# Four buffers of TensorE operands placed 64 bytes further along in SBUF

## The reference

```python
    h = rmsnorm(x, norm_ffn[l])
    gt, up = jnp.split(h @ w_ffn_in[l], 2, axis=-1)
    x = x + ((jax.nn.silu(gt) * up) @ w_ffn_out[l]).astype(x.dtype)
return rmsnorm(x, norm_final)
```

## The kernel before

| operand | role | before |
|---|---|---|
| `h_hi`, `h_lo` | moving | on the line |
| `t_hi`, `t_lo` | moving | on the line |
| weight rings `w_hi`, `w_lo` (sums, output weights) | stationary, then moving | on the line |
| `wa22` blocks, both sets (product 2) | stationary | on the line |
| `wa_lo`, set 0 | stationary | half off (`H + 8192`) |
| `wa_hi`, `wa_lo`, set 1 | stationary | half off (`H`, `H + 14464`) |
| `wa_hi`, set 0 | stationary | on the line (`Dd + 32768`) |
| `a_hi`, `a_lo` | stationary | on the line |

## Time and profile before

### The profile page before, as it was taken

How to read it: one execution, slowest core, us unless ns; L and a number is a source line. 1 busy time by engine, 2 the same in 40 slices (tenths; PEclk the granted TensorE clock), 3 DMA queues, 4 the chain that set the end, 5 groups by cost and what they waited for, 6 DMA issues and landing times.

```text
span 783.5 us, 12585 instructions
## 1 busy us (share of the span) xinstructions
PE 775.8 (99%) x4994; PEld 676.3 (86%) x4994; DVE 485.5 (62%) x920; ACT 327.2 (42%) x597; POOL 154.6 (20%) x111
## 2 busy tenths in 40 slices
PE   9999999999999999999999999999999999999996
PEld 7878899889878787788888988999999999888885
DVE  5935432555776767656625668898788876332347
ACT  5212055254446666653313624444444443222145
POOL 1300100000000000002200185876666650000000
PEclk9999999999999999999999999999999999999999
DMA  6941336250311111036331731334333335333302
GB/s 217 339 154 54 108 61 155 57 167 4 109 54 55 55 55 41 23 98 190 108 108 54 229 94 55 108 109 117 104 104 107 108 109 192 130 108 107 107 1 107
DMA packets 101286, 83.50 MB, mean 107 GB/s; under 512 B 16960, under 2 KB 94832, under 8 KB 101232
## 3 DMA queue, kind: packets, MB, share of 16 engines
q1 hardware_dynamic: 100992, 82.46, 35.2%
q10 hardware_dynamic: 240, 0.29, 0.1%
HBM read 77.44 MB, written 5.29 MB: 106 GB/s over the span
## 4 chain that ended last, share of the span: by engine, by line
PE 99%; DMA 0%; ACT 0%; DVE 0%; issue 0%; ACTq 0%; DVEq 0%
PE bank L1681 28%; PE bank L1682 28%; PE bank L1683 28%; PE bank L1914 2%; PE bank L1933 2%; PE bank L1901 2%; PE bank L1815 1%; PE bank L1856 1%; PE bank L1837 1%; PE bank L1778 1%; PE bank L1722 1%; PE bank L1705 1%; PE bank L1728 1%; PE bank L1928 1%; PE bank L1731 0%; PE bank L1868 0%
## 5 line engine op out<-in xcount | busy, mean ns | idle before, releaser
L1028 DVE TENSOR_TENSOR w_lo<-w_raw,w_hi 128x2048 fp32r<-128x2048 f32 (+2 forms) x29 | 64.5, 2224 | 79.5 <-ACT w_hi L677 79.4
L1681 PE MATMUL bank<-n_hi,w_hi 128*128 128x512 f32 x272 | 108.8, 400 | 0.0
L1683 PE MATMUL bank<-n_hi,w_lo 128*128 128x512 f32 x272 | 106.1, 390 | 0.0
L1682 PE MATMUL bank<-n_lo,w_hi 128*128 128x512 f32 x272 | 106.0, 390 | 0.0
L677 ACT CAST w_hi<-w_raw 128x2048 fp32r<-128x2048 f32 (+2 forms) x29 | 53.6, 1848 | 61.8 <-PE bank L1683 51.1
L1681 PE MATMUL bank<-w_hi,a_hi 128*128 128x512 f32 (+1 forms) x180 | 69.3, 385 | 0.0
L633 POOL TENSOR_TENSOR n_lo<-merge_tmp,n_hi 128x512 fp32r<-128x512 f32 x8 | 10.4, 1298 | 298.2 <-ACT n_hi L859 298.2
L1682 PE MATMUL bank<-w_lo,a_hi 128*128 128x512 f32 (+1 forms) x180 | 69.2, 384 | 0.0
L1683 PE MATMUL bank<-w_hi,a_lo 128*128 128x512 f32 (+1 forms) x180 | 69.2, 384 | 0.0
L1681 PE MATMUL bank<-w_hi,n_hi 128*128 128x256 f32 (+2 forms) x192 | 62.1, 323 | 0.0
L1683 PE MATMUL bank<-w_hi,n_lo 128*128 128x256 f32 (+2 forms) x192 | 61.4, 320 | 0.0
(11 more groups left out here) (268 smaller groups left out, 1927.4 us busy)
## 6 DMA issues: line engine op xcount, KB each, us to landing
w_raw<-in_w_ffn_in_dram SPq DMA_DIRECT2D x44, 512.0 KB, 5.0
w_raw<-in_w_in_dram SPq DMA_DIRECT2D x37, 512.0 KB, 4.9
w_raw<-in_w_ffn_out_dram SPq DMA_DIRECT2D x22, 512.0 KB, 4.2
w_raw<-in_w_out_dram SPq DMA_DIRECT2D x8, 512.0 KB, 4.1
w_raw<-in_w_in_dram SPq DMA_DIRECT2D x12, 256.0 KB, 4.7
xs<-in_x_dram SPq DMA_DIRECT2D x4, 512.0 KB, 4.6
wck_k<-in_w_ck_dram SPq DMA_DIRECT2D x1, 2048.0 KB, 11.8
wck_v<-in_w_cv_dram SPq DMA_DIRECT2D x1, 2048.0 KB, 15.0
```

What stands on the lines that cost most here:

```text
L1028: dve.tensor_tensor(wlo[u % 2][:, 0:n], raw[u % 2][:, 0:n], whi[u % 2][:, 0:n].bitcast(F32), ALU.subtract).then_inc(lo_done, 1)
L1681: pe.matmul(dst, w[0], x_[0], start=start, stop=False)
L1682: pe.matmul(dst, w[0], x_[1], start=False, stop=False)
L1683: return pe.matmul(dst, w[1], x_[0], start=False, stop=stop)
```

## The change

`a_hi`, `a_lo`, `t_lo`, `t_sums` and set 0 of `wa_hi` move up by 64 bytes, `t_hi` moves down by 64 bytes, and a tile that nothing used (`tanh_g`) is dropped. All that move go from "on the line" to "half off". No instruction, wait or place in an engine's order differs, on any engine.

```diff
-        ahi, alo = (at(f"a_{k}", [2, 2, S], A + 45056 + o, F32R) for k, o in (("hi", 0), ("lo", 8192)))
-        tg = at("tanh_g", [2, S], A + 61440)
+        ahi, alo = (at(f"a_{k}", [2, 2, S], A + 45120 + o, F32R) for k, o in (("hi", 0), ("lo", 8192)))
...
         ahi7 = [[at(f"wa_hi{j}", [KC, P], o, F32R), at(f"wa22_hi{j}", [4, P], o2, F32R)]
-                for j, o, o2 in ((0, Dd + 32768, G + 4608), (1, H, G + 8704))]
+                for j, o, o2 in ((0, Dd + 32832, G + 4608), (1, H, G + 8704))]
...
-        thi = at("t_hi", [4, 4, 256], C, F32R)
-        tlo = at("t_lo", [4, 4, 256], A + 45056, F32R)
-        t7 = at("t_sums", [4, 4, 256], A + 45056)
+        thi = at("t_hi", [4, 4, 256], C - 64, F32R)
+        tlo = at("t_lo", [4, 4, 256], A + 45120, F32R)
+        t7 = at("t_sums", [4, 4, 256], A + 45120)
```

## The result

The changed kernel takes 785.13 us (median of 17 runs) where the kernel before takes 784.07 (17 runs beside it): ratio 1.0017, interval 1.0010 to 1.0025. It is about 1 us slower; 9 us less was forecast. Device time lies 1.8 us above the span (785.01 against 783.2 in the profiled execution after), not 0.6 as I had it. Executions of one kernel also differ early on: the profiled one of before was already 1.5 us behind that of after at its 49th matmul (13.28 against 11.82 us) and 1.4 us at the start of unit 5 (487.38 against 485.94), so stages are compared here and not spans.

The account below looks back on a forecast made before the run. PE was taken to bound the kernel, its time set by matmul count times start-to-start distance. Terms 5.5 + 0.9 + 3.6 - 0.5 - 0.2 - 0.1 = 9.2 us took the median from 784.14 to 774.9 us, range 773.8 to 779.0.

Parts of the forecast that it names:

- PE bounds, and only the distance counts: Both stretches: PE, busy 99% of the span, hardly waits; time is number of matmuls times distance from start to start.
- The rule read from rows 3 to 5: Stationary and moving operand at different halves of 128 bytes cost 113.3 ns a matmul, at the same half 120 ns.
- Mixtures, 5.5 us: Products 2, 4, 5 and 6: t_hi and t_lo half off save 6.7 ns on each of 816 matmuls, 5.5 us.
- `wa_hi` of set 0, 0.9 us: Products 1 and 3 of the 8 even units: 128 matmuls become like odd units', 6.7 ns less each, 0.9 us.
- `a`, 3.6 us less: Second half, a_hi and a_lo: 540 matmuls save 6.7 ns each, 3.6 us, bounded between 0 and 7.2.
- Given back: Gains lost waiting: 0.5 us at unit 6's product 4, behind ACT's copy, and 0.2 us at the end of unit 21.
- slower: Rival, 0.03: moving operands half off need 64 bytes more reading; mixtures lose 5.5 us, total 785.1, or 790.6 at 13.3 ns.
- Waits take more of it: Rival, 0.05: DVE's chain gains less on PE, unit 7's 0.92 us is used up, about 1.5 us more stays: 776.4.
- Wide matmuls do not respond: Rival, 0.08: the step belongs to 256 columns alone, so the second half's 3.6 us are missing: 778.5.
- only the stationary address counts: Rival, 0.11: moving the mixtures does nothing; 0.9 + 3.6 less about 0.1 leaves 4.4 us gain: 779.7.
- address is indifferent: Rival, 0.03: the distance does not depend on operand addresses, as independent read ports imply; time stays 784.1.
- The sum: Whole kernel: 9.2 us less, 774.9; with the step sizes and losses between none and 1.5 us, 774.0 to 776.5.

Follow-up runs that it names:

- the replay: No layer: TensorE alone runs a unit's 84 matmuls at the kernel's addresses in 13 layouts; kernel's unit times matched within 0.01 us, 9.60 to 9.61 with weight sums at 64.
- experiment 3: No layer: TensorE alone, streams of 24 matmuls per pair of places and width; 256 columns 113.3 to 120.0 ns, 512 columns 226.7 (both alike) or 233.5 (stationary 64 further).
- experiment 5: No layer: TensorE alone, streams of 24 at the kernel's steps, hi and lo parts moved separately; 120 all alike, 113.3 stationary 64, 192, 118.3 moving 192, 64; 233.3 ns for 512 columns.
- experiment 10: No layer: TensorE alone, streams of 48 behind different streams or with alternating places; same matmuls, weights at 64: 117.7 ns behind a 120 ns stream, 113.2 behind a 113.3 one.
- experiment 4: Kernel before with only wa_hi of set 0 moved half off: 783.4 us, ratio 0.9997; first stage 169.27 us.
- experiment 2: Changed kernel with t_hi, t_lo and t_sums back on the line, t_lo blocks spaced out: 785.5 us, ratio 1.0015; stages 168.41 and 123.22 us.
- experiment 8: As experiment 7, with the wa22 blocks of both sets and m1_u4_u3 also 64 bytes further: 777.34 us, ratio 0.9917; first stage 163.01 us.
- experiment 1: Changed kernel with a_hi and a_lo back on the line, t_lo blocks 4224 bytes apart: 783.32 us, ratio 0.9993 to the kernel before; second half 120.09 us.
- experiment 7: Kernel before with the weight sums 64 bytes further along and wa_hi of set 0 half off: 778.61 us, ratio 0.9924; first stage 164.28 us.
- experiment 9: As experiment 1, but t_lo's blocks 4352 bytes apart, a multiple of 256: 782.03 us, ratio 0.9975 to the kernel before; stages 167.89 and 120.09 us.

## Why the prediction was wrong

- *PE bounds, and only the distance counts*: right. PE is 97% of the chain after, no instruction moved, and the replay gives the kernel's units to 0.01 us.
- *The rule read from rows 3 to 5* is the step that failed: "where the stationary and the moving operand lie at different halves of 128 bytes a matmul costs 113.3 ns". At 256 columns the rows showed three layouts only: hi and lo of `wa` at 192 and 64 from the moving operand modulo 256, the two at 0 and 192 (even units), and all alike. I made a rule with period 128 of them. In its place the runs show that the place modulo 256, of hi and lo apart, and the stream ahead matter (experiments 3, 5, 10): stationary 64, 192 gave 113.3, moving 192, 64 gave 117.8.
- *Mixtures, 5.5 us*: mis-sized. `t_hi` moved down and `t_lo` up, and this pair settles at 118.1 on average, 1.9 ns below 120: 816 x 1.9 = 1.5 us.
- *`wa_hi` of set 0, 0.9 us*: right in kind, 0.6 alone (experiment 4), since three of a product's twelve matmuls pass before it is at its own pace.
- *`a`, 3.6 us less*: wrong sign. I bounded it between 0 and 7.2 of gain, "since equal excess at both widths speaks for a cost per matmul". Measured: 516 matmuls 6.3 ns **slower** (3.25 us), 24 narrow ones 5.8 faster (1.9 in experiment 2 at the same places). Equal excess was no evidence that it could be removed; 226.7 is the least that any place gave at 512 columns (to 0.1 ns). The bound excluded a loss with no row at that width, and that alone cost the sign.
- *Given back*: right. ACT's copy in unit 6 starts 13.96 us after the stage's start before (501.34 - 487.38) and after (499.90 - 485.94), so it is anchored as I said. After the change PE starts product 4 there 0.56 us after the matmul ahead, 0.40 before, so what little it had gained by then, 0.17 us, was lost. In experiment 8, where the expected pace was reached, it is 0.97 us, 0.86 of it waiting, about the 0.8 forecast. ACT's copy and PE's two matmuls after the change:

```profile
499.90 0.37 ACT L914 COPY m_u_u<-bank 128x256 f32<-128x256 f32 x1 [3.98 <-DVE bank L1518]
...
499.85 0.28 PE L1682 MATMUL bank<-h_hi,wa_lo 128*128 128x256 f32 x1
500.41 0.36 PE L1680 MATMUL bank<-t_hi,w_hi 128*128 128x256 f32 x1 [0.29 <-ACT m_u_u L914]
```

- *The rivals*: "slower" gave 785.1 us, which is the time that came, but by luck: the mixtures were to lose and gained, `a` was to gain and lost. "Waits take more of it" did not happen: the wait in unit 6 is the only one of PE's that grew by more than 0.04 us. "Wide matmuls do not respond" falls with experiments 1 and 3, "only the stationary address counts" with 3 and 5 (moving operand alone at 112: 113.3 ns), "address is indifferent" with all of them. By the rule of independent read ports, in the Trainium skill's "TensorE: Matmul & The Clock Gate", section "What happens when you issue a matmul", a weight load takes no read bandwidth from the running matmul. The distance that does not depend on the places, which the prediction drew from it, is not what these traces show: with TensorE alone, the two operands' places change it by 6.7 ns (113.3 to 120.0, 226.7 to 233.3). What in the chip makes the difference is not shown.
- *The sum*: the 5.6 us forecast for the first stage, and more, were there to be had, but by moving stationary blocks and not the mixtures: 169.85 - 163.01 = 6.8 us in experiment 8. Moving both parts of `t` the same way, to 192, would have come part of the way: by the replay's 9.73 and 9.84 us a unit, 9 odd and 8 even ones take 166.3 us (an estimate without unit 6's wait; not run in the kernel). And the upper end of the forecast's own spread, 776.5, does not follow from losses of up to 1.5 us: 784.1 - 10.0 + 1.5 = 775.6.

## What to carry to other kernels

In a stream where every fp32r matmul has its own weight load, operand addresses were worth up to 6% at 256 columns here (120.0 against 113.3 ns): replay the stream on TensorE alone for a dozen layouts, at the kernel's real addresses and in its real order, before any tile is moved. Read places modulo 256 bytes, of hi and lo apart, per width, and never carry a sign from one width to another without a row of that width. A stage's gain can be undone by another stage that uses the same shift, so compare stage by stage.

## What was not expected of the hardware

Some paces come again and again: of the 208 combinations with 256 columns in experiment 5, 94 settled at 117.8 ns, 18 at 120.0, 12 at 116.7 and 4 at 113.3, the least. The 64 with 512 columns lay between 226.7 and 235.5. From 256 to 512 columns, all alike, the distance grows by 226.7 - 120.0 = 106.7 ns; the least distances are 6.7 and 13.3 ns above one and two times that. Streams settle into a repeating pattern after up to some ten matmuls, and a product of 12 is short enough to feel it: product 7, not touched by the change, went from 120.0 to about 118.8, and is back at 120 only for its last few matmuls. At 128 columns the distance stayed at 111.6 ns for all eight places of the stationary block that were tried.

DVE's split of the weight sums took 1346 ns before and 1712 after, at unchanged addresses, and about as much in experiments 1, 7, 8 and 9 (1700 to 1712), but 1345 in 2 and 4; POOL had 102.24 and 100.27 us in the first stage. The kept traces show with what it goes. One split takes 1.2 us, or 2.3 in some cases, and in all eight kernels every long one started while one of POOL's weight sums was running: 4 of 34 splits before, 15 after. In one unit before, DVE starts at 574.87 and POOL at 574.88, and DVE takes 1.22 us and POOL 2.37; after, POOL starts at 572.51 and DVE at 572.53, and POOL takes 1.29 us and DVE 2.35. In these two units the one that starts second takes about 1.1 us longer, and a shift of some 30 ns between them moves that from POOL to DVE. PE did not wait for it after the change: its one wait that grew by more than 0.04 us, in unit 6, is for a copy that stayed where it was.
